# Expert loads of 2 MB and expert outputs added inside the loop, in an encoder layer on one Trainium2 core

## What is computed

```
p_group = softmax(xf @ w_rg); g_idx = argmax(p_group)       # one of 4 groups
top_v, top_i = top_k(fine[g_idx], 2)                         # two experts of its 8
gate = p_group[g_idx] * softmax(top_v)
...
yb = (silu(xblk @ w1[e]) * (xblk @ w3[e])) @ w2[e]           # for each expert e
y  = zeros.at[slot_tok].add(yb * slot_w)                     # back to the tokens
x  = x + y;  out = rms_norm(x, norm_final)
```

## Time and profile before

| | us |
|---|---|
| median of 3 runs (lowest, highest) | 2090.63 (2085.91, 2092.15) |
| the profiled execution, device time | 2092.59 |
| its span in the profile | 2090.7 |
| TensorE busy | 1931.8 (92%) |
| VectorE busy | 648.9 (31%) |
| ScalarE busy | 519.2 (25%) |
| mean granted TensorE clock | 0.957 of full |

### The profile page before, as it was taken

The page is one execution under the profiler, slowest core; times in us unless marked ns, Lnnn a source line. Parts: engine busy times, 40 slices in busy tenths (PEclk is TensorE's granted clock), DMA queues, the critical chain, the costliest instruction groups (busy, mean ns, idle before and its releaser), DMA issues.

```text
span 2090.7 us, 25445 instructions
## 1 busy us (share of the span) xinstructions
PE 1931.8 (92%) x10296; PEld 1302.5 (62%) x10296; DVE 648.9 (31%) x970; ACT 519.2 (25%) x735; POOL 50.5 (2%) x54
## 2 busy tenths in 40 slices
PE   6999999899999999999699899999999999998987
PEld 6889799799777889888434344443443443444344
DVE  3644455888545544343500000000000000000003
ACT  4444343634334443333110000000000000000001
POOL 0000000022210000000000000000000000000000
PEclk9999999999999999999799999999999999999999
DMA  7454444334664545248079999999999999999950
GB/s 266 166 175 152 137 159 160 121 122 144 123 157 155 187 146 177 81 168 327 2 309 394 414 415 400 418 405 414 407 413 404 416 411 410 401 411 410 410 222 40
DMA packets 134622, 556.65 MB, mean 266 GB/s; under 512 B 15408, under 2 KB 15640, under 8 KB 84248
## 3 DMA queue, kind: packets, MB, share of 16 engines
q1 hardware_dynamic: 133528, 553.55, 68.5%
q0 software_dynamic: 1024, 2.10, 1.4%
HBM read 553.51 MB, written 2.10 MB: 266 GB/s over the span
## 4 chain that ended last, share of the span: by engine, by line
PE 75%; DMA 16%; DVE 4%; ACT 2%; issue 2%; SPq 1%; POOL 0%; DVEq 0%; ACTq 0%
DMA arena<-in_moe_w_dram 15%; PE ps L836 13%; PE ps L859 11%; PE ps L847 6%; PE ps L527 6%; PE ps L528 6%; PE ps L529 6%; PE ps L521 5%; PE ps L522 5%; PE ps L523 5%; PE ps L811 1%; PE ps L933 1%; PE ps L670 1%; PE ps L489 1%; PE ps L922 1%
## 5 line engine op out<-in xcount | busy, mean ns | idle before, releaser
L836 PE MATMUL ps<-arena 128*64 128x512 f32 x2048 | 509.0, 642 | 72.8 <-DMA arena<-in_moe_w_dram 70.8
L1370 DVE TENSOR_TENSOR w_lo<-arena,w_hi 128x1024 fp32r<-128x1024 f32 x264 | 319.2, 1252 | 295.8 <-ACT w_hi L996 295.2
L836 PEld LDWEIGHTS ps<-arena 128*64 128x64 f32 x2048 | 147.0, 146 | 380.2 <-issue 251.2
L996 ACT ACTIVATE w_hi<-arena 128x1024 fp32r<-128x1024 f32 x264 | 264.3, 1051 | 335.3 <-PE ps L523 176.9
L859 PE MATMUL ps<-arena 128*64 128x512 f32 x1024 | 225.2, 592 | 0.5 <-DVE arena L1877 0.5
L859 PEld LDWEIGHTS ps<-arena 128*64 128x64 f32 x1024 | 73.3, 137 | 146.4 <-issue 145.8
L521 PE MATMUL ps<-x_hi,w_hi 128*128 128x256 f32 x512 | 147.1, 287 | 6.9 <-DVE w_lo L1370 6.9
L522 PE MATMUL ps<-x_lo,w_hi 128*128 128x256 f32 x512 | 146.3, 286 | 0.0
L523 PE MATMUL ps<-x_hi,w_lo 128*128 128x256 f32 x512 | 146.2, 286 | 0.0
L847 PEld LDWEIGHTS ps<-stack,arena 128*128 128x128 f32 x512 | 121.9, 328 | 26.0 <-issue 26.0
L847 PE MATMUL ps<-stack,arena 128*128 128x64 f32 x512 | 126.4, 401 | 0.0
(11 more groups left out here) (335 smaller groups left out, 2631.3 us busy)
## 6 DMA issues: line engine op xcount, KB each, us to landing
arena<-in_moe_w_dram SPq DMA_DIRECT2D x384, 1024.0 KB, 12.5
arena<-in_w_in_dram SPq DMA_DIRECT2D x52, 1024.0 KB, 4.9
arena<-in_xa_wk_dram SPq DMA_DIRECT2D x16, 1024.0 KB, 5.1
arena<-in_xa_wv_dram SPq DMA_DIRECT2D x16, 1024.0 KB, 5.1
arena<-in_w_out_dram SPq DMA_DIRECT2D x16, 1024.0 KB, 5.1
arena<-in_xa_wq_dram SPq DMA_DIRECT2D x16, 1024.0 KB, 5.1
arena<-in_xa_wo_dram SPq DMA_DIRECT2D x16, 1024.0 KB, 5.1
arena<-in_x_dram SPq DMA_DIRECT2D x2, 1024.0 KB, 6.0
```

The lines of the kernel that those rows point to most:

```text
L836: last = mm(ps[rows_, m, :], xe[:, ECH * i + c, :], ring_up[m][i][:, c, :], start=(i == 0 and c < 2), stop=(i == ECH - 1 and c >= 2))
L996: fn(hi_ring[(2 * n + u) % 4][:], ring_a[i][:, 2 * u:2 * u + 2, :], ACT.Copy).then_inc(S["w_hi"], 1)
L1370: V.tensor_tensor(w_lo[i][:, 2 * u:2 * u + 2, :], ring_a[i][:, 2 * u:2 * u + 2, :], hi_ring[(2 * n + u) % 4][:].bitcast(F32), ALU.subtract ...
```

## The change

Two things change, and one moves.

1. The twelve weight loads of 1 MB of an expert, with 8 KB in each partition, become six of 2 MB, with 16 KB in one run in each partition. Two neighbouring chunks have one load and one semaphore. A load waits until both chunks of its pair have been used, and TensorE waits for both to have landed before the first of them.
2. `turn_y`, `ysT`, `selgT`, and the products and additions after the loop are gone. In their place the gate weight of each slot is multiplied into the SiLU part (`sgw`), the 64 x 2048 result of `down` is split into a rounded part and its remainder (`d_hi` on ScalarE, `d_lo` on VectorE, two tiles each), and `comb(n, q)` multiplies each with a 0/1 matrix `pick` (64 slots x 256 tokens, built by two VectorE instructions for each expert). There are four `comb` in a block, one behind each `up(n, 1, i)`, each of four products of 64 x 128 by 64 x 512 in the float32r format. VectorE adds each result, 128 x 1024, to `h` in the loop.
3. The tokens of an expert (`xe`) have two buffers and are copied two blocks ahead. The rows of slots and gates (`slot_rows`: six products) are made behind block 0. `fgain` is loaded before the loop, and SyncE waits for `slot_rows` before that, since `fgain` takes the place of the selection tiles.

```diff
             def load_up(e, n, m, i):
-                    sp.wait_ge(S["up_used0" if m == 0 else "up_used1"], n * ECH + (i + 1 - ECH))
-                sp.dma_start(ring_up[m][i], up_chunk(e, m, i)).then_inc(s_up[m][i], 16)
+                    sp.wait_ge(S["up_used0" if m == 0 else "up_used1"], n * ECH + (i + 2 - ECH))
+                sp.dma_start(pair_up[m][i // 2], up_chunk(e, m, i)).then_inc(s_up[m][i // 2], 16)
             def load_down(e, n, i):
-                    sp.wait_ge(S["dn_used"], n * ECH + (i + 1 - ECH))
-                sp.dma_start(ring_dn[i], down_chunk(e, i)).then_inc(s_dn[i], 16)
+                    sp.wait_ge(S["dn_used"], n * ECH + (i + 2 - ECH))
+                sp.dma_start(pair_dn[i // 2], down_chunk(e, i)).then_inc(s_dn[i // 2], 16)
...
+            sp.wait_ge(S["row_pe"], 1)
+            sp.wait_ge(S["tab_dve"], 3)
+            sp.dma_start(fgain, ins["norm_final"].rearrange("(a d) -> a d", a=1).to_broadcast([P, D])).then_inc(S["fgain_in"], 16)
             with sp.Fori(1, NE) as e:
                 load_expert(e, e)
...
-            def turn_y(n):
...
+            def comb(n, q, par, b0=6, behind=0):
+                u, j = q // 2, q % 2
+                if q == 0:
+                    pe.wait_ge(S["pick_all"], n + 1)
+                if j == 0:
+                    pe.wait_ge(S["ev_hi"], n * 2 + (u + 1))
+                    pe.wait_ge(S["ev_lo"], n * 2 + (u + 1))
+                if not (isinstance(n, int) and 4 * n + q <= behind):
+                    pe.wait_ge(S["c_add"], n * 4 + (q - behind))
+                for part in (d_hi, d_lo):
+                    for b in range(2):
+                        rows_ = slice(EB * b, EB * (b + 1))
+                        last = mm(ps[:, b0 + b, :], pick[par][rows_, j * P:(j + 1) * P], part[u][rows_, :],
+                                  start=(part is d_hi), stop=(part is d_lo))
+                last.then_inc(S["c_pe"], 1)
             def block_n(n, back, par):
...
-                up(n, 1, 0)
-                up(n, 1, 1)
-                if back is not None:
-                    turn_y(back)
-                up(n, 1, 2)
-                up(n, 1, 3)
+                for i in range(ECH):
+                    up(n, 1, i, par)
+                    if back is not None:
+                        comb(back, i, 1 - par)
...
+            block_n(0, None, 0)
+            slot_rows()
+            block_n(1, 0, 1)
...
-                        last = mm(ps[:, 4 + n % 4, u * P:(u + 1) * P], ysT[:, k_, s * P:(s + 1) * P], ident[:], start=True, stop=True)
...
-                        last = mm(ps[:, m % 4, :], selgT[:, s, j * P:(j + 1) * P], ys[:, s, g * 512:(g + 1) * 512],
-                                  start=(s == 0), stop=(s == SLOTS // P - 1))
...
+            def add(n, q, b0=6):
+                u, j = q // 2, q % 2
+                hv = h[:, j, 1024 * u:1024 * (u + 1)]
+                dve.wait_ge(S["c_pe"], n * 4 + (q + 1))
+                V.tensor_tensor(hv, flat(ps[:, b0:b0 + 2, :]), hv, ALU.add).then_inc(S["c_add"], 1)
+            def block_n(back, s_back, par, then):
+                gating(back, s_back)
+                if then:
+                    tokens(back + 2, start_of(back + 2), par)
+                picked(back, par)
+                down_lo(back)
+                for q in range(4):
+                    add(back, q)
```

More of the change, by code:

```diff
@@ L239, in program @@
         xsT = arena(16, KT, SLOTS + EB)
[L240 to L246, removed]
+        d_hi = [at_r(f"d_hi{u}", 52 + 2 * u, [P, 512]) for u in range(2)]
+        d_lo = [at_r(f"d_lo{u}", 56 + 2 * u, [P, 512]) for u in range(2)]
+        rows_s = arena(60, 2, T)
+        pick = [at_r(f"pick{u}", 62 + u, [P, T]) for u in range(2)]
+        fgain = arena(64, D)
+        ptmp = arena(84, T)
+        xe = [arena(88, KT, EB), arena(92, KT, EB)]
+        wrow = arena(96, SLOTS + EB)
+        sg, sgw = arena(98.5, ECH, EB), arena(200, ECH, EB)
+        hT = arena(201, ECH, EB)
+        up_ev = arena(100, 2, FF)
         sel_r, sel_g, sel_t = arena(64, NT, SLOTS), arena(68, NT, SLOTS), arena(78, SLOTS)
@@ L816, in _, with slot_rows, up @@
             pe.wait_ge(S["r_dve"], 4)
[L817 to L821, removed]
+            mm(ps[:, 6, 0:3 * OVB], ones, flat(ov_rhs), start=True, stop=True).then_inc(S["r_pe"], 1)
+            def slot_rows():
+                for k_, slot_ in enumerate((slot0, slot1)):
+                    for j in range(NT):
+                        mm(ps[:, 5, (2 * k_ + j) * P:(2 * k_ + j + 1) * P], slot_[:, j:j + 1].to_broadcast([P, P]), ident[:], start=True, stop=True)
+                pe.wait_ge(S["tab_dve"], 2)
                 for j in range(NT):
-                    last = mm(bank(4 + s // 2, 2, NT, P)[:, s % 2, j, :], sel_g[:, j, s * P:(s + 1) * P], ident[:], start=True, stop=True)
-            last.then_inc(S["sg_pe"], 1)
-            def up(n, m, i):
+                    last = mm(ps[:, 4, :], ones, sel_g[:, j, :], start=(j == 0), stop=(j == NT - 1))
+                last.then_inc(S["row_pe"], 1)
+            def up(n, m, i, par):
                 if i == 0:
@@ L861, in down, with block_n @@
                 last.then_inc(S["dn_used"], 1)
-            def turn_y(n):
[L865 to L876, removed]
+            def comb(n, q, par, b0=6, behind=0):
[13 more added lines that the diff above has]
+                last.then_inc(S["c_pe"], 1)
+            def block_n(n, back, par):
+                up(n, 0, 0, par)
+                up(n, 0, 1, par)
                 if back is not None:
                     sums(back)
-                up(n, 0, 2)
-                up(n, 0, 3)
+                up(n, 0, 2, par)
+                up(n, 0, 3, par)
                 if back is not None:
@@ L894, in finish_n @@
                     down(n, i)
[L895 to L904, removed]
+                for q in range(4):
+                    comb(n, q, par, 6 - 6 * (q % 2), 1)
+            block_n(0, None, 0)
+            slot_rows()
+            block_n(1, 0, 1)
+            with pe.Fori(0, NE // 2 - 1) as e:
+                block_n(e * 2 + 2, e * 2 + 1, 0)
+                block_n(e * 2 + 3, e * 2 + 2, 1)
+            finish_n(NE - 1, 1)
             pe.wait_ge(S["tab_dve"], 3)
@@ L1248, in silu, with down_hi @@
                 fn(flat(sg), flat(bank(2, ECH, EB)), ACT.Silu).then_inc(S["e_sg"], 1)
-            def down_out(n):
+            def down_hi(n):
                 act.wait_ge(S["dn_used"], n * ECH + ECH)
[L1252 to L1262, removed]
+                for u in range(2):
+                    if not (isinstance(n, int) and n == 0):
+                        act.wait_ge(S["c_pe"], n * 4 - 2 + 2 * u)
+                    fn(d_hi[u][:], ps[:, 4 + u, :], ACT.Copy).then_inc(S["ev_hi"], 1)
             def block_n(n, back):
                 if back is not None:
-                    s_back = start_of(back)
                     silu(back)
@@ L1892, in finish_n @@
[L1892 to L1907 removed]
+                V.tensor_tensor(flat(hT), flat(bank(3, ECH, EB)), flat(sgw), ALU.mult).then_inc(S["e_h"], 1)
@@ new lines, in down_lo @@
+            def down_lo(n):
+                for u in range(2):
+                    dve.wait_ge(S["ev_hi"], n * 2 + (u + 1))
+                    if not (isinstance(n, int) and n == 0):
+                        dve.wait_ge(S["c_pe"], n * 4 - 2 + 2 * u)
+                    V.tensor_tensor(d_lo[u][:], ps[:, 4 + u, :], d_hi[u][:].bitcast(F32), ALU.subtract).then_inc(S["ev_lo"], 1)
+            def add(n, q, b0=6):
[3 more added lines that the diff above has]
+                V.tensor_tensor(hv, flat(ps[:, b0:b0 + 2, :]), hv, ALU.add).then_inc(S["c_add"], 1)
@@ new lines, in block_n, with finish_n @@
+            def block_n(back, s_back, par, then):
[4 more added lines that the diff above has]
+                down_lo(back)
+                for q in range(4):
+                    add(back, q)
+            def finish_n(n, s, par):
+                gating(n, s)
+                picked(n, par)
+                down_lo(n)
+                for q in range(4):
+                    add(n, q, 6 - 6 * (q % 2))
```

215 lines of the change are left out of this document (91 added, 124 removed).

## The result

The changed kernel takes 2154.68 us (median of 4 runs, 2152.82 to 2157.99) where the one before takes 2091.39: ratio 1.0309, 95% interval 1.0286 to 1.0333. It is 63 us slower; 71 were forecast, 2162 us. The profiled execution took 2152.82 us, its span is 2151.0.

The account below looks back on a forecast made before the run. Neither full engine alone but a ring of waits through w2's reload and w1's landing was taken as the bound; +95.4 loop, +11.5 start, -35.5 end make +71.4 on 2092.59, 2164, less 2.0 for the median: 2162 us, range 2088 to 2195.

Parts of the forecast that it names:

- The ring: In the loop: w2's reload waits longer, TensorE waits for more w1 behind it; block 34.0 us, 3.29 more, +95.4 us.
- the start: Before block 2: fgain waits for slot_rows and delays expert 1's loads; block 2 starts at 1105.2, not 1093.74: +11.5 us.
- the end: From the last down to the end of the span: 27.7 us in place of 65.5; -35.5 us after a longer last block.
- the transfer leg: In the loop, w2's first reload to w1's landing: six MiB, between 17.1 and 18.8 us, taken as 17.95.
- TensorE's leg: In the loop, first up to w2's release: 16.07 us, with the pair after the pause at the lower clock (5.28).
- The later release (1.72 us): In the loop: w2's reload waits for two down chunks, 3.43 us and not 1.72, added in full to the block.
- the first rival: In the loop: pause stays, clock does not fall or falls late; block 32.3 us, sum +20, 2111 us; chance 0.22.
- The low end of this rival: In the loop: the first rival with the lower transfer leg, 17.1 us; block 31.4, sum -8, 2083 us.
- The combination: In the loop: turn_y goes, sixteen products with their turns cost 3.4 to 5.3 us, taken 4.3, hidden in the pause.
- the rival that it outgrows the pause: In the loop: four comb take 10 us, no pause is left, block 34.9 us, 2193 us in all; chance 0.07.
- The rival of faster loads: In the loop: loads set the pace, fewer longer ones run faster; block 29.5 to 30.7, 2049 us at 30.1; chance 0.14.

Follow-up runs that it names:

- 1 MB loads: The changed kernel with its six 2 MB loads for each expert turned back into twelve of 1 MB; 2061.4 us, ratio 0.9857 to the kernel before.

## Why the prediction was right, and where its sizes were off

**The ring.** Right, and shown from both sides: pairing the load that TensorE waits for costs 2.31 us a block, and taking the reload of `w2` out from in front of `w1` takes the whole loss away. The block came to 33.63 us, 34.0 forecast. Of the 11.1 us between the 71.4 forecast and the 60.3 between the spans, the loop has 11.5; the start cost 2.1 more than forecast and the end gained 1.7 more. In the loop the transfer leg was put 0.68 us too high and TensorE's leg 0.29 too low, so a part of the closeness is luck.

**The transfer leg** was put at 17.95 us, between 17.1 and 18.8; it is 17.27. The upper bound came from an idle start with single releases, 1.7 us apart, and carried their 1.35 us; the changed kernel lets `w2` out two by two and hardly pays them. The measured leg is 0.2 us above the lower bound. The kernel before pays for its single releases too (364 GB/s behind the first reload), although its DMA engines are still full there (408 GB/s in the 3 us up to it, mean of 30 blocks). That its leg of 16.4 us equals the 16.31 of the idle start was read as an empty queue; a small stock, and the slow microseconds behind it, are what the trace shows.

**The later release (1.72 us)** was the step that failed as a cause, though the sum came out near. It was added in full. With pairs in `w2` alone the later release costs 0.16 us a block, beside pairs in `w1` 0.63: what it adds to one leg it takes for the most part from the other. Two reasons are in the traces; how much each gives was not separated. Released two by two the loads get through faster (414 GB/s against 376 in the five microseconds, 0.45 of the 1.38 us). And old loads are served while the release waits: in the 3 us up to it the DMA engines move 381 GB/s, 423 with single releases. In its place `w1` alone carries 2.31 of 2.94 us; `w2` and `w3` alone have 0.16 and 0.17, and the rest appears only together.

**TensorE's leg** of 16.07 us with the lower clock: measured 16.36. The pair behind the pause took 5.07 on average (5.28 forecast), the second half of `w1` 3.78 (3.49), since the clock fell again behind `sums` in 8 of 30 blocks, and the first reload went out 3.64 us after the start of `down` (3.43). The clock fell behind the pause in 25 of 30 blocks; blocks in which it did not take 31.7 us, for which the rival had 32.3. So the first rival lived in one block of six, not in the mean. Filling the pause gave 1.4 us of clock back in the first half of `w1` and lost 0.5 in the second; the block gained 1.07. The low end of this rival was worked out as a sum of -8, 2083 us; with its own terms, 0.85 us in each of 29 blocks and once in the start, it is -6 and 2085, which changes nothing.

**The combination** was costed at 3.4 to 5.3 us. It takes 1535.56 - 1534.90 = 0.66 us from the first product of a `comb` to the next `up`. With the turns it is a little more: one `up` chunk and one `comb` follow each other every 1537.43 - 1534.90 = 2.53 us, and a chunk alone takes 3.49 / 2 = 1.75, so a `comb` costs 0.78 us and the four 3.1, under the range. Two products on the two row halves need 0.33 us, where one by one they would take 0.46: the halves overlap. The two turns between 64 and 128 rows add at most 0.12 us beside the 0.66, not the 0.4 read from the earlier stage; what of the 0.66 is theirs the rows do not tell. The Trainium skill ("TensorEngine Tiling (Array Packing)", Key Properties) says that row tiles work side by side; these rows agree. All of it lies in the pause, as forecast (1 MB loads: 30.69 against 30.73), and the rival that it outgrows the pause had nothing for it.

**The start** cost 13.6 us, 11.5 forecast. Block 0 began at 1042.90 (1043.6), `fgain` went out at 1061.03 (1060.6), block 1 began at 1070.73 (1071.2). The 2 us are in TensorE's leg of block 1: from 1070.73 to the first reload at 1089.20 it took 18.47 us, not 16.07. Behind the pause of 9.73 us its first pair took 6.36 us and the second half of `w1` 4.55. The transfer leg behind it was 18.2 us, 17.95 forecast.

**The end** gained 37.2 us, 35.5 forecast. The four additions take 4.62 us (5.3), and VectorE's skipped iterations 3.9 (5.3, read from TensorE).

**The rival of faster loads** had a real core of 1.5%: 428 GB/s against 422. It is worth 12 us where the transfers are the bound; in this ring no run shows a gain from it. Its premise, that the 364 GB/s of the reload stage are a cost of short loads, falls: 1 MB loads moved 422 there when `w2` was released two by two, and 421 to 422 when they stood behind `w1`. The Trainium skill ("DMA: Bandwidth & Descriptors", Bandwidth) gives 341 GB/s for a transfer of 1 MB issued from GpSimd and 425 for 16 MB. Queued loads of 1 MiB, issued from SyncE, reach 422 here, so what its table charges a transfer of 1 MB is not paid in a full queue.

## What to carry to other kernels

When two engines look full and neither has slack, follow one buffer round: who frees it, what stands in front of its reload in the queue, who waits for its landing. A larger load makes its first user wait for its last byte, so do not enlarge the load whose landing is awaited (2.31 us a block here). Enlarging the others brought nothing while the ring was closed: 5 and 6 us more. So first of all ask whether a reload that could go out stands behind one that can't. Once the ring is open, the larger loads are worth their small gain.

## What the runs showed that was not expected

- Loads let out one by one, 1.7 us apart, with few others queued, moved 366 GB/s from 2 to 7 us behind the first, two by two 422, at the same size of 1 MB and nearly the same shown share (0.99 and 1.01 in the windows). That the DMA engines were full up to then (1 MB loads everywhere) did not help: 376. A long queue did: 422.
- A stretch of products with 64 columns, TensorE busy all through (3.90 of 3.90 us), was followed by the lower clock level (0.51 granted) just as a pause was. It did not take a pause: with `w1` issued ahead of `w2` TensorE waited for no `w1`, and the second half of `w1` was slow in 15 of 30 blocks; behind the pauses of the changed kernel in 8 of 30. What decides in which blocks it happens was not settled.
- 2.6 us more work in each block made the kernel 1.5% faster (2154.7 to 2121.5 us; by the ratios to the kernel before on each chip 1.8%).
